# Two 512-column layer norm products moved into the middle of two runs of 8-column state products, in the RWKV stage of the sampled tokens

## What is computed

```
def wkv_scan(r, decay, k, v, kk, a, s0):
    def step(S, inp):
        r_t, w_t, k_t, v_t, kk_t, a_t = inp
        sk = jnp.einsum('bhij,bhj->bhi', S, kk_t)
        S = S * w_t[:, :, None, :] - sk[..., None] * (kk_t * a_t)[:, :, None, :] + v_t[..., None] * k_t[:, :, None, :]
        return S, jnp.einsum('bhij,bhj->bhi', S, r_t)
...
    mean = jnp.mean(o, axis=-1, keepdims=True)
    var = jnp.mean(jnp.square(o - mean), axis=-1, keepdims=True)
    o = ((o - mean) * lax.rsqrt(var + LN_X_EPS)).reshape(B, T, RWKV_WIDTH) * W['rwkv_ln_gain'] + W['rwkv_ln_bias']
    bonus = jnp.sum(r_h * k_h * W['rwkv_r_k'], axis=-1, keepdims=True) * v_h
    o_rwkv = ((o + bonus.reshape(B, T, RWKV_WIDTH)) * g).astype(x.dtype)
```

## Time and profile before

| what | value |
|---|---|
| median of 3 timed executions | 1726.77 us (1726.29 to 1730.38) |
| profiled execution, its own time | 1729.89 us |
| its span, first to last instruction | 1728.1 us |
| PE busy | 1673.5 us, 97% |
| DVE busy | 951.8 us, 55% |
| ACT busy | 737.8 us, 43% |
| POOL busy | 710.8 us, 41% |
| mean granted clock of TensorE | 0.991 |

### The profile page before, as it was taken

How to read it: one execution, slowest core, us unless ns; L and a number is a source line. 1 busy time by engine, 2 the same in 40 slices (tenths; PEclk the granted TensorE clock), 3 DMA queues, 4 the chain that set the end, 5 groups by cost and what they waited for, 6 DMA issues and landing times.

```text
span 1728.1 us, 41702 instructions
## 1 busy us (share of the span) xinstructions
PE 1673.5 (97%) x16684; PEld 1589.3 (92%) x16684; DVE 951.8 (55%) x1479; ACT 737.8 (43%) x1226; POOL 710.8 (41%) x912
## 2 busy tenths in 40 slices
PE   6899999999899999999999999999999899999999
PEld 6899999999889998987798989898999799999999
DVE  5836547366864546543575463627455945637363
ACT  5544536355524242423253443435234543526442
POOL 4554645554432222311132322324255563646543
PEclk9999999999999999999899999999999999999999
DMA  4353433423432333322055454446353352342513
GB/s 183 118 191 110 133 111 122 158 75 138 152 140 85 103 122 121 113 75 90 32 213 187 174 186 161 175 153 242 136 217 121 139 197 83 121 153 103 192 62 107
DMA packets 57498, 237.31 MB, mean 137 GB/s; under 512 B 7520, under 2 KB 8160, under 8 KB 55904
## 3 DMA queue, kind: packets, MB, share of 16 engines
q1 hardware_dynamic: 49440, 218.35, 35.8%
q10 hardware_dynamic: 7872, 16.37, 2.5%
HBM read 216.93 MB, written 71.76 MB: 167 GB/s over the span
## 4 chain that ended last, share of the span: by engine, by line
PE 83%; DVE 8%; issue 3%; POOL 2%; ACT 2%; DVEq 1%; DMA 0%; ACTq 0%; POOLq 0%
PE ps L405 28%; PE ps L834 23%; PE ps L844 15%; PE ps L1438 3%; POOL w_lo L392 2%; PE ps L2390 1%; PE ps L2434 1%; PE ps L2565 1%; PE ps L2490 1%; PE ps L2512 1%; DVE T_lo L973 1%; PE ps L2474 1%; DVE B_lo L973 1%; PE ps L2505 0%; ACT w_hi L385 0%
## 5 line engine op out<-in xcount | busy, mean ns | idle before, releaser
L392 POOL TENSOR_TENSOR w_lo<-w_raw,w_hi 128x256 fp32r<-128x256 f32 x384 | 320.4, 865 | 678.3 <-ACT w_hi L385 678.3
L405 PE MATMUL ps<-h_hi,w_hi 128*128 128x288 f32 x1232 | 289.5, 317 | 19.7 <-POOL w_lo L392 14.9
L405 PE MATMUL ps<-h_hi,w_lo 128*128 128x288 f32 x1232 | 265.1, 297 | 0.0
L405 PE MATMUL ps<-h_lo,w_hi 128*128 128x288 f32 x1232 | 264.6, 297 | 0.0
L405 PEld LDWEIGHTS ps<-h_hi,w_hi 128*128 128x128 f32 x1232 | 199.4, 190 | 42.4 <-POOL w_lo L392 16.0
L405 PEld LDWEIGHTS ps<-h_lo,w_hi 128*128 128x128 f32 x1232 | 199.5, 190 | 0.0
L405 PEld LDWEIGHTS ps<-h_hi,w_lo 128*128 128x128 f32 x1232 | 199.5, 190 | 0.0
L817 POOL TENSOR_TENSOR ring_lo<-raw,ring_hi 128x256 fp32r<-128x256 f32 (+1 forms) x197 | 147.3, 774 | 113.4 <-ACT ring_hi L798 112.5
L385 ACT ACTIVATE w_hi<-w_raw 128x1024 fp32r<-128x1024 f32 x96 | 101.7, 1059 | 115.5 <-PE ps L405 95.7
L834 PE MATMUL ps<-T_hi,ring_hi 128*128 128x288 f32 x396 | 118.1, 298 | 11.1 <-ACT u L1061 8.7
L1244 DVE SCALAR_TENSOR_TENSOR x<-ps,x 128x576 f32<-128x576 f32 x64 | 48.5, 758 | 139.5 <-PE ps L844 138.2
(11 more groups left out here) (453 smaller groups left out, 3953.9 us busy)
## 6 DMA issues: line engine op xcount, KB each, us to landing
w_raw<-in_w SPq DMA_DIRECT2D x122, 512.0 KB, 3.5
raw<-in_w SPq DMA_DIRECT2D x48, 512.0 KB, 4.8
kv<-in_kc SPq DMA_DIRECT2D x32, 576.0 KB, 6.2
kv<-in_vc SPq DMA_DIRECT2D x32, 576.0 KB, 7.4
cache_out<-in_cache SPq DMA_DIRECT2D x28, 576.0 KB
raw<-in_w_down SPq DMA_DIRECT2D x32, 384.0 KB, 3.5
w_raw<-in_w_down SPq DMA_DIRECT2D x16, 384.0 KB, 3.7
gates<-gate_out ACTq DMA_DIRECT2D x16, 288.0 KB, 3.0
```

The costliest lines, as they stand in the source:

```text
L392: last = nc.gpsimd.tensor_tensor(w_lo[par_][:, c], w_raw[par_][:, c], w_hi[par_][:, c].bitcast(F32), ALU.subtract)
L405: last = nc.tensor.matmul(ps[:, b + c, 0:HC], w[par_][:, wk], a[:, k, c * HC:(c + 1) * HC], start=(first and k == 0), stop=(end and k == n ...
```

## The change

`ln_gate(pe, 1)` is issued between the 32nd and 33rd of the 64 products of run 1, at (ct, b, h) = (2, 0, 0), and no longer behind the run. `ln_gate(pe, 2)` is issued at the same place of run 2. Their waits for `rsqrt_read` move with them. `ln_centre(pe, 2)` and `ln_centre(pe, 3)` stay behind the runs. The other engines' programs are the same.

```diff
--- before.py
+++ after.py
@@ -2039,11 +2039,12 @@
             pe.wait_ge(sem("s_dve"), 5)
             pe.wait_ge(sem("s_states"), 16)
             for ct, b, h in ((ct, b, h) for ct in range(CT) for b in range(DB) for h in range(2)):
+                if (ct, b, h) == (2, 0, 0):
+                    ln_gate(pe, 1)
                 c = slice(64 * ct + 8 * b, 64 * ct + 8 * b + 8)
                 last = nc.tensor.matmul(ps[rows_of(h), 6, c], SST[rows_of(h), ct, 64 * b:64 * b + 64], SXK[rows_of(h), c],
                                         start=True, stop=True)
             last.then_inc(sem("smat"), 1)
-            ln_gate(pe, 1)
             ln_centre(pe, 2)
             fill(2)
             pe.wait_ge(sem("s_act"), 6)
@@ -2059,11 +2060,12 @@
                     nc.tensor.matmul(o, SUU[:, hc(ct, h)], SNB[:, mc(ct, h)], start=(ct == 0), stop=False, skip_group_check=True)
                     nc.tensor.matmul(o, TOS[3][:, hc(ct, h)], SNK[:, mc(ct, h)], start=False, stop=True, skip_group_check=True)
             for ct, b, h in ((ct, b, h) for ct in range(CT) for b in range(DB) for h in range(2)):
+                if (ct, b, h) == (2, 0, 0):
+                    ln_gate(pe, 2)
                 c = slice(64 * ct + 8 * b, 64 * ct + 8 * b + 8)
                 last = nc.tensor.matmul(ps[rows_of(h), 5, c], SST[rows_of(h), ct, 64 * b:64 * b + 64],
                                         SV[rows_of(h), ct, 3, 8 * b:8 * b + 8], start=True, stop=True)
             last.then_inc(sem("smat"), 1)
-            ln_gate(pe, 2)
             ln_centre(pe, 3)
             for ct in range(CT):
                 pe.wait_ge(sem("s_spread"), ct + 1)
```

## The result

The changed kernel takes 1735.32 us (median of 5, 1733.57 to 1737.16), the kernel before, measured beside it, 1729.98 us (5 executions, of which three are those of the table ahead of the prediction). The ratio is 1.0032, with a 95% interval of 1.0021 to 1.0044: 5.3 us slower. The kernel before was measured in 100 further executions beside the experiments, in four groups with medians of 1729.5 to 1730.2; the 1726.77 us of the first three was a low sample.

The account below looks back on a forecast made before the run. Bound by PE's own low-clock work between 831 and 842 and, behind run 2, the chain ScalarE, VectorE, PE. Terms +0.1, +0.2 and +1.2 gave +1.5 us on the median 1726.77: 1728.3, range 1724.3 to 1731.5.

Parts of the forecast that it names:

- Part 1 without the clock (+0.1): ln_gate(1) inside run 1: wait already met, ScalarE's copy covered, only a change of product shape costs, 0.1 us.
- The clock term of run 1 (+1.2): Run 1: gate and centring split, so the clock rises later and fills run low; +1.2 us, range 0 to 1.6.
- Part 2 without the clock (+0.2): ln_gate(2) inside run 2: VectorE's 0.91 us idle is given back by the run's delay; +0.2 us with shape change.
- I take the low end: Run 2: of +0.2 to +1.2 us, the low end was chosen because the clock stood at full until 850.48.
- can't grow: Behind run 2, from PE's release at 854.35 on: any shift passes on undiminished, with no slack to absorb it.
- rival C: Run 2: clock falls ahead of the gate, stays low over the wait behind the centring; +6.3 us, 1733.1; chance 0.07.
- Rival A: Run 1: the gate in the middle holds the clock at 2.4 GHz, -3.1 us there; sum -2.9, 1723.9; chance 0.22.
- Rival B: Clock does what it did, or PE's queue order makes no difference; only +0.3 us, 1727.1; chance 0.28.
- the stretch from run 1's start to PE's resumption: From 831.46 to PE's resumption after run 2: shorter than 22.9 us would mean the forecast's sign was wrong.
- L2295 was to come about 1 us later: VectorE's add behind run 2 was to stand about 1 us after its old place against the run's start.
- PE was to be idle 2 us or more: Behind run 2's centring, PE was to idle 2 us or more before the first state product.
- The low-clock time around run 1: Around run 1, more than 6.8 us at the low clock was expected, with the centring alone at the low clock.

Follow-up runs that it names:

- Gate 2 alone: Only ln_gate(2) moved into the middle of run 2, run 1 as in the kernel before; ratio 1.0019 to the kernel before.
- The delayed kernel: The kernel before with five 128x128 copies on ScalarE ahead of the stage's barrier, nothing else changed; 1733.8 us, ratio 1.0017.
- the pair inside: Against the kernel before, ln_gate and ln_centre together mid-run: in both runs, 1.0010; in run 1 only, one fill moved behind ln_centre(3), 0.9998.
- gate 1 alone: Only ln_gate(1) moved into run 1, run 2 as in the kernel before: ratio 1.0021; with five ScalarE copies ahead of the stage, 1.0039.

## Why the prediction was wrong

**The sign was forecast, the size not.** +1.5 us was forecast and +5.3 measured, and 1735.32 is outside 1724.3 to 1731.5. Of the 7.0 us between 1728.3 and 1735.3, 3.2 are the base: the forecast was put on the median of three executions, 1726.77, though the profiled execution (1729.89) was, as it turned out, the better sample. The text named their spread and then used the median alone. The remaining 3.8 are the change.

**Part 1 without the clock (+0.1)** was right as far as it can be seen: waits met, copy covered, nobody late. **The clock term of run 1 (+1.2)** had its mechanism right and its size a little low, where the clock fell early. It had the low stretch made longer by the split pair, over the gate, the 64 products, the centring and the fills. That is what three profiles show, 10.2 us low in place of 6.8, and run 2 starts 1.8 us later there (the end of the range was 1.6). In the changed kernel's own profile the early fall didn't come, and run 1 gained 1.3 us; by the table above, that the early fall was missing is the luck of the execution and no effect of the gate. The Trainium skill (TensorE: Matmul & The Clock Gate, Part 1) says that activity releases the throttle; these traces agree in so far as every rise behind a low stretch at run 1 came while products of 288 or 512 columns ran. But its summary's counsel to keep TensorE busy without gaps isn't enough here: all falls in run 1 came with PE busy.

**Part 2 without the clock (+0.2)** was right in each step. The add starts 0.63 us behind the run (853.11 to 853.74), as before; the gating 0.51 behind that; the spreads end 2.1 after its start. The 0.91 us was given back as worked out. **The step that failed is the choice behind it**: "I take the low end, as the clock in run 2 stood at full until 850.48", together with the statement on PE's release behind run 2 that a shift passes on undiminished and "can't grow". The prediction had worked out for run 1 that a split pair makes the low stretch longer, and put that at nothing for run 2. Gate 2 alone shows what stands in its place: with the fall at its old distance of 4.0 us, the low stretch is 10.2 us in place of 3.4, PE resumes 1.1 us later and loses 2.4 more behind the resumption, and over 11 executions it costs 3.2 us. The shift did grow.

In the changed kernel's profile the clock fell earlier still, at 847.12, ahead of the gate, and that is **rival C**, with its price: forecast +2.5 at the resumption and +2.2 behind it, profile +3.0 and +2.1. The rival's sum was 6.3 with 1.6 for run 1, where the profile has -1.3. Its chance, 0.07, was too low, and the reason given for it was that in the trace the second fall came only at the end of run 2. That was one execution's fall, treated as if it stood at that product. The delayed kernel shows that it doesn't, and gate 2 alone that the loss comes even where it does. The prediction noticed that the clock differs between executions and widened each case by a microsecond, in place of asking to which work the low stretch could move.

**Rival A** (the gate in the middle holds the clock) isn't borne out: in three of five profiles with the gate there the clock fell early, and a run without gate or pair in it stayed at full clock too. Its gain of 3.1 us is in the profiles with the pair inside (10.5 to 7.6) and, less a fill, in that of the unchanged run; over many executions nothing of it was left. **Rival B** (the clock as before) is out: 12.3 us more at the low clock.

Of the signs named, L2165 stands behind the add with no wait for the gate, and the stretch from run 1's start to PE's resumption is longer (24.6 us against 22.9). L2295 was to come about 1 us later against run 2's start and came 3.8 later, and PE was to be idle 2 us or more and was idle 1.19; both miss by the low clock over run 2. The low-clock time around run 1, which was to be more than 6.8 us, is 3.4 in that profile and 10.2 in the three others.

What stays open: how the 5.6 us divide. The profile has 0.1 to 0.2 of order and the rest clock, the executions 3.6 to 6.1 for the clock, so an order share of up to 2 us isn't excluded. That gate 1 alone costs its 3.3 us by the longer low stretch at run 1 is what its delayed profile shows (+1.8 us there, +1.9 up to the gate of the last piece against the delayed kernel before); that the nine slower executions without the delay did the same is likely and not shown.

## What to carry to other kernels

Where narrow products make TensorE's clock fall, the place of the fall isn't a property of the instruction at which one trace shows it, and whether it comes at all can differ between two executions of the same instructions. Before pricing a reordering, price the low stretch at every piece of work that it could come to lie on, and ask which of them sit on the path; moving wide work forward into a narrow run takes it away from behind the run, and in this kernel the clock then came back later (10.2 us low in place of 6.8 or 3.4). And compare mean granted clock and time over many executions: a gain of 3 us in one profile was nothing in eleven.

## What was not expected of the hardware

- A pure delay of 1.7 us ahead of the stage cost 3.5 us (means). In its profile the clock was low for 3.4 us more at the stage's start, and behind run 2 its low stretch lay over the state products and was 10.2 us long in place of 3.4, which had been mostly covered by VectorE's work.
- Behind the same instructions, with run 1 starting at 831.07 us in one execution and 831.16 in another, the clock fell 1.9 us into the run in the first and stayed full until 846.57 in the second.
- One program gave two groups of times, 1728.9 to 1729.3 and 1738.0 to 1738.6 us, with mean clocks of 0.993 to 0.994 and 0.986.
